# Identity products added into free PSUM banks on a TensorE-bound block of three layers, with banks taken ahead of the operands

## The reference, cut to what matters

```
S = S * w_t + (S a_t) b_t^T + v_t k_t^T ;   y_t = S r_t
```

## Time and profile before

| | |
|---|---|
| three runs | 4579.30, 4583.82, 4586.74 us, median 4583.82 |
| profiled execution | 4590.26 us, span 4588.4 us |
| granted TensorE clock, mean of the span | 0.847 |
| PE busy | 3906.6 us, 85% |
| DVE, ACT, POOL busy | 1815.2, 1229.7, 163.9 us |
| DMA | 219.39 MB, mean 48 GB/s |

### The profile page before, as it was taken

The page is one execution under the profiler, slowest core; times in us unless marked ns, Lnnn a source line. Parts: engine busy times, 40 slices in busy tenths (PEclk is TensorE's granted clock), DMA queues, the critical chain, the costliest instruction groups (busy, mean ns, idle before and its releaser), DMA issues. The chain is left out here.

```text
span 4588.4 us, 67812 instructions
## 1 busy us (share of the span) xinstructions
PE 3906.6 (85%) x29441; PEld 2998.5 (65%) x29441; DVE 1815.2 (40%) x2944; ACT 1229.7 (27%) x1936; POOL 163.9 (4%) x116
## 2 busy tenths in 40 slices
PE   5888888897888898999777667779799999877888
PEld 4667666677777798998455444558677877334543
DVE  3443444424444435343344344453553344322231
ACT  2222212212333222222222333322222221244230
POOL 0000000000000101000011001120000000000000
PEclk8777777759988798999887778779999999867987
DMA  3000000001111132332101001013223332201110
GB/s 128 16 16 15 16 16 16 16 2 56 29 32 33 45 104 65 92 90 67 37 24 37 28 24 32 22 44 97 69 75 95 93 92 87 69 10 32 37 33 23
DMA packets 58554, 219.39 MB, mean 48 GB/s; under 512 B 6608, under 2 KB 6608, under 8 KB 57616
## 3 DMA queue, kind: packets, MB, share of 16 engines
q1 hardware_dynamic: 57168, 211.37, 15.2%
q0 software_dynamic: 1088, 3.67, 0.2%
HBM read 210.83 MB, written 4.19 MB: 47 GB/s over the span
## 5 line engine op out<-in xcount | busy, mean ns | idle before, releaser
L385 PE MATMUL psum<-arena 32*32 32x32 f32 (+16 forms) x16392 | 1378.6, 265 | 529.8 <-DVE arena L321 152.1
L385 PE MATMUL psum<-arena,ring 128*128 128x264 f32 (+3 forms) x5152 | 1664.7, 414 | 18.3 <-DVE arena L330 11.8
L385 PEld LDWEIGHTS psum<-arena 32*32 32x32 f32 (+9 forms) x16392 | 988.6, 153 | 922.7 <-issue 332.3
L385 PE MATMUL psum<-arena,arena 128*128 128x264 f32 (+1 forms) x6336 | 1394.1, 328 | 74.7 <-DVE arena L321 37.3
L385 PEld LDWEIGHTS psum<-arena,ring 128*128 128x128 f32 (+2 forms) x5152 | 939.4, 199 | 371.6 <-issue 278.0
L385 PEld LDWEIGHTS psum<-arena,arena 128*128 128x128 f32 x6336 | 1004.2, 192 | 192.5 <-issue 62.1
L314 ACT ACTIVATE arena<-psum 128x512 f32<-128x512 f32 (+11 forms) x561 | 258.1, 460 | 1287.0 <-PE psum L385 1176.8
L321 DVE TENSOR_TENSOR ring<-ring,arena 128x1024 fp32r<-128x1024 f32 (+1 forms) x280 | 333.2, 1190 | 488.4 <-ACT arena L314 484.3
L321 DVE TENSOR_TENSOR arena<-arena 128x528 f32<-128x528 f32 (+9 forms) x700 | 336.8, 481 | 350.0 <-ACT arena L311 208.7
L314 ACT ACTIVATE arena<-ring 128x1024 fp32r<-128x1024 f32 (+1 forms) x280 | 286.7, 1024 | 558.5 <-PE psum L385 480.5
L321 DVE TENSOR_TENSOR arena<-arena,psum 88x192 f32<-88x192 f32 (+4 forms) x428 | 193.4, 452 | 585.9 <-PE psum L385 578.9
(11 more groups left out here) (24 smaller groups left out, 701.6 us busy)
## 6 DMA issues: line engine op xcount, KB each, us to landing
ring<-in_w SPq DMA_DIRECT2D x368, 512.0 KB, 3.5
ring<-in_w SPq DMA_DIRECT2D x24, 256.0 KB, 2.7
arena<-in_x SPq DMA_DIRECT2D x2, 2112.0 KB, 14.7
arena<-in_con SPq DMA_DIRECT2D x1, 3576.0 KB, 11.3
out<-arena SPq DMA_DIRECT2D x1, 2048.0 KB, 6.3
arena<-in_par SPq DMA_DIRECT2D x1, 1988.0 KB, 15.5
skew<-arena POOLq DMA_DIRECT2D x4, 320.0 KB, 2.6
arena<-skew POOLq DMA_DIRECT2D x4, 256.0 KB, 2.9
```

Source lines behind the costliest of these rows:

```text
L385: self.last_ins = self.eng.matmul(out, l, r, start=start, stop=stop, skip_group_check=skip)
```

## The change

A counter `idle` is kept while the program is written out; nothing of it runs on the chip. `mm` adds what a product is taken to last, the larger of 25 and n/2.4, and takes off n x rows/128, where n is the number of columns, times four for F32. `tr` adds 100. `wait_ge` adds 300 for each wait that is issued. The counter never goes below -1500 in `mm`. `bank` calls `warm` once the bank is free: while the counter is over 300 it issues a product of the 128x128 identity with itself into the first 128 columns of that bank, which the next real product overwrites. Each such product lowers the counter by 512 - 213.3 = 298.7.

The second part moves calls of `bank` ahead of waits on operands, in some 35 places: the wait on the bank, and what `warm` issues, then stand before the wait on the operand.

```diff
     def bank(self, n, *emptied):
...
         self.book.put(("bank",) + emptied, b)
+        self.warm(b)
         return b
+
+    def warm(self, b):
+        while self.idle > 300:
+            self.mm(self.ps[:, 512 * b:512 * b + 128], self.ident, self.ident)
+
+    def wait_ge(self, sem, n):
+        if self.seen.get(sem.num, 0) < n:
+            self.idle += 300
+        super().wait_ge(sem, n)
...
     def mm(self, out, l, r, start=True, stop=True, skip=False):
+        rows, n = l.shape[0], math.prod(r.shape[1:]) * (1 if r.dtype == F32R else 4)
+        self.idle = max(-1500, self.idle + max(25, n / 2.4) - n * rows / 128)
         self.last_ins = self.eng.matmul(out, l, r, start=start, stop=stop, skip_group_check=skip)
 
     def tr(self, out, a):
         n = a.shape[0]
+        self.idle += 100
         self.last_ins = self.eng.transpose(out, a, self.ident[0:n, 0:n])
...
     def prep(hp):
         for i, nme in enumerate("rkv"):
             s, w = P.slab((3 + 3 * hp + i) * SLAB, "rw_proj", hp, i)
+            b = P.bank(2, "rw_sh", hp, i)
             P.wait_ge(*landed(K, s))
-            b = P.bank(2, "rw_sh", hp, i)
             P.keep(b, 2)
...
-    def blocks(done, emptied, l, r):
+    def blocks(done, emptied, l, r, *needs):
         b = P.bank(1, *emptied)
+        for event in needs:
+            P.wait_ge(*at(*event))
...
         for l in (2, 4, 8, 16):
             for hh in range(2):
                 u = m.unit[hh]
-                P.wait_ge(*at("rw_mask", l, hp, hh))
-                P.wait_ge(*(at("rw_xt", l // 2, hp, hh)))
-                blocks(("rw_inv", "Y", l, hp, hh), ("rw_yp", l, hp, hh), u.M0 if l in (2, 8) else u.M1, u.Xp)
+                blocks(("rw_inv", "Y", l, hp, hh), ("rw_yp", l, hp, hh), u.M0 if l in (2, 8) else u.M1, u.Xp,
+                       ("rw_mask", l, hp, hh), ("rw_xt", l // 2, hp, hh))
             P.advance()
             for hh in range(2):
                 u = m.unit[hh]
-                P.wait_ge(*at("rw_yp", l, hp, hh))
-                blocks(("rw_inv", "Z", l, hp, hh), ("rw_x", l, hp, hh), u.XTp, u.Yp)
+                blocks(("rw_inv", "Z", l, hp, hh), ("rw_x", l, hp, hh), u.XTp, u.Yp, ("rw_yp", l, hp, hh))
                 blocks(("rw_inv", "ZT", l, hp, hh), ("rw_xt", l, hp, hh), u.Yp, u.XTp)
...
```

More of the change, by code:

```diff
@@ L356, in __init__ @@
         self.free, self.nbank, self.kept, self.slabs = [None] * 8, 0, set(), []
+        self.idle = 0.0
     def bank(self, n, *emptied):
@@ L1315, in project @@
         yield
+        b = P.bank(2, "df_V", hd)
         P.wait_ge(*at("df_v", hd))
-        b = P.bank(2, "df_V", hd)
         for j, (t0, tw) in enumerate(TK):
@@ L1352, in values @@
         nb = 2 if i == 4 else 1
+        b = P.bank(nb, "df_wt", hd, i)
         P.wait_ge(*at("df_w", hd, i))
-        b = P.bank(nb, "df_wt", hd, i)
         m0 = 512 * b if i == 4 else 512 * b + 128 * i
@@ L1864, in glin @@
         s, w = P.slab(off, *done)
+        b = P.bank(1, *emptied)
         P.wait_ge(*landed(K, s))
-        b = P.bank(1, *emptied)
         P.keep(b)
@@ L1886, in v_tile, with four @@
         P.drop(b)
-    def four(done, emptied, l, r):
+    def four(done, emptied, l, r, *needs):
         b = P.bank(1, *emptied)
+        for event in needs:
+            P.wait_ge(*at(*event))
         for J in J4:
@@ L1902, in pe_mixers @@
     s, w = P.slab(w0, "gd_small")
+    b = P.bank(1, "gd_lr")
     P.wait_ge(*landed(K, s))
-    b = P.bank(1, "gd_lr")
     for k in range(8):
@@ L1916, in delta @@
         yield
+        b = P.bank(1, "gd_to")
         P.wait_ge(*at("gd_g"))
-        b = P.bank(1, "gd_to")
         P.mm(bk(b)[:, 0:16], c["triu"], m.G["g"])
@@ L1922, in delta @@
         yield
+        b = P.bank(1, "gd_ct")
         P.wait_ge(*at("gd_bec"))
-        b = P.bank(1, "gd_ct")
         P.tr(bk(b)[0:16, 0:128], m.G["cu"])
@@ L1935, in delta @@
             yield
+            b = P.bank(1, "gd_diff", hd)
             P.wait_ge(*at("gd_ct"))
-            b = P.bank(1, "gd_diff", hd)
             for j in range(4):
@@ L1942, in delta @@
             yield
-            P.wait_ge(*at("gd_qi", hd))
-            four(("gd_kk", hd), ("gd_A", hd), U.k, U.k)
+            four(("gd_kk", hd), ("gd_A", hd), U.k, U.k, ("gd_qi", hd))
             four(("gd_kq", hd), ("gd_M", hd), U.k, U.q)
@@ L1954, in delta @@
             yield
+            b = P.bank(1, "gd_AT", hd)
             P.wait_ge(*at("gd_A", hd))
-            b = P.bank(1, "gd_AT", hd)
             for J in J4:
@@ L1988, in delta @@
             yield
+            b = P.bank(1, "gd_yp", 64, hd)
             P.wait_ge(*at("gd_m0", hd))
-            b = P.bank(1, "gd_yp", 64, hd)
             for j in range(4):
@@ L1995, in delta @@
             yield
+            b = P.bank(1, "gd_x64", hd)
             P.wait_ge(*at("gd_yp", 64, hd))
@@ L2013, in delta @@
                 if j:
+                    b = P.bank(1, "gd_us", j, hd)
                     P.wait_ge(*at("gd_wt", hd))
                     P.wait_ge(*at("gd_s", j, hd))
[L2016 removed]
                     P.mm(bk(b)[:, 0:128], U.wT[:, J], so)
@@ L2049, in decay_attention @@
         yield
+        b = P.bank(1, "la_ks", r)
         P.wait_ge(*at("la_qi", r))
-        b = P.bank(1, "la_ks", r)
         for J in J4:
@@ L2093, in linear @@
             off += 6 * SLAB
+            b = P.bank(1, "la_pre", r)
             P.wait_ge(*at("gd_lr"))
-            b = P.bank(1, "la_pre", r)
             P.mm(bk(b), p["glaw2"][0:16, 128 * r:128 * r + 128], m.LR[0:16])
@@ L2671, in pe_experts @@
             if e == 0:
+                b = P.bank(1, "r_ct")
                 P.wait_ge(*at("r_w"))
-                b = P.bank(1, "r_ct")
                 for j in range(4):
@@ L2943, in scores @@
             R, (k0, W) = slice(64 * r, 64 * r + 64), keys_of(kind, i)
+            b = P.bank(1, "fx_e", t, r, i)
             P.wait_ge(*at("fx_qk", t, "k"))
-            b = P.bank(1, "fx_e", t, r, i)
             s_ = bk(b)[:, 0:W]
@@ L2962, in values @@
             k0, W = keys_of(kind, i)
+            b = P.bank(1, "fx_a", t, r, i)
             P.wait_ge(*at("fx_p", t, r, i))
-            b = P.bank(1, "fx_a", t, r, i)
             for j in range(W // 128):
@@ L3012, in sticks @@
                 W = 512 - 128 * j
+                b = P.bank(1, "st_z", t, r, j)
                 P.wait_ge(*at("fx_k", t))
-                b = P.bank(1, "st_z", t, r, j)
                 P.mm(bk(b)[:, 0:W], d.k[R, J4[j]], d.q[R, 128 * j:512])
@@ L3019, in sticks @@
                 W = 512 - 128 * j
+                b = P.bank(1, "st_a", t, r, j)
                 P.wait_ge(*at("st_lk", t, r, 3))
-                b = P.bank(1, "st_a", t, r, j)
                 P.mm(bk(b)[:, 0:W], c["slo"], m.Lk[j][:, 0:W])
@@ L3052, in tables @@
         for i in range(8):
+            b = P.bank(1, "tb_v", i)
             P.wait_ge(*at("tb_rb", i))
-            b = P.bank(1, "tb_v", i)
             P.mm(bk(b), m.rb[0:32, 0:128], c["oh"][0:32])
```

16 lines of the change are left out of this document (5 added, 11 removed).

## The result

The changed kernel takes 4643.2 us (median of 4634.8, 4638.8, 4647.5 and 4650.0) against 4582.2 us of the kernel before in the same comparison: ratio 1.0131, 95% interval 1.0110 to 1.0152. It is slower by 61 us. The profiled execution took 4634.8 us, the lowest of its four; that of before, 4590.3, was the highest of its own. So the two traces differ by 45 us and the medians by 61. The two traces say where 45 us went.

A forecast was written before the change was run, and what follows sets the result against it. PE was taken to bound the kernel, busy 85% of the span, with 31% at half clock. Terms 25 + 6 + 8 + 0 + 0 = +39 us on 4590.3 gave 4629, as a median 4623 us; range 4550 to 4655.

The forecast's parts named there:

- Count: Whole kernel: 286 identity products, 572 records; 16 in each of head pairs 1 to 6, placed by the counter's rule.
- Price of one: One identity product: 0.22 us at full speed, 0.44 at half, plus 0.15 for a group among small blocks.
- Head pairs 1 to 6: RWKV's middle head pairs: each net 4.1 us longer, six times 25 us; bounds 14 and 38.
- give-back: Head pairs 1 to 6: work pushed behind the clock's rise runs in half the time, returning 2.2 us each.
- Head pair 0: First RWKV head pair: 29 products, nearly all at full speed, cost 6 us; bounds 4 and 9.
- Head pair 7: Last RWKV head pair: 68 products, levels at full speed but longer; +8 us, ends +14 and -4.
- What I doubted: Head pair 7: w2, u and chain, 26 us at half speed, might keep a raised clock; perhaps 10 us would go.
- Mixers: Mixers: 76 products fill waits and lift the clock, but shorten no round; 0 us, bounds +8 and -5.
- Moves of `bank`: `bank` calls moved ahead of operand waits: cost nothing, since both waits must end before the first product in either order.
- Rival (a): Gram products: clock held at full speed there, 10 us a head pair, 70 in seven; total 4553 us; chance 0.17.
- Rival (c): Nothing is given back in head pairs 1 to 6 and head pair 7 stays slow: +61, 4645 us; chance 0.15.
- what it would show: Signs: 30013 PE records, middle head pairs 4 us longer, chain and gram at 0.50, decay rounds 4.4 to 4.6 us at 1.00.

The follow-up runs named there:

- few rows: Changed kernel's 272 products in the same places, each with 32 rows of the identity instead of 128: 4699.5 us, ratio 1.0266 to the kernel before.
- gram few: Kernel before, moved banks, ten 32-row identity products ahead of the first `Ak` per head pair, no counter products: 4593.4 us against 4581.9, ratio 1.0025.
- no last: Changed kernel without the products from the first level to the last piece of the inverse in the last head pair: 4626.7 us, ratio 1.0109 to before.
- moves only: Changed kernel with counter and moved `bank` calls but no identity product issued: 4580.7 us against 4579.1 of the kernel before, ratio 1.0009.
- no mixers: Changed kernel without the products in the three mixers of block 2: 4623.3 us, ratio 1.0107 to the kernel before.
- gram fill: Kernel before, moved banks, ten full-row identity products ahead of the first `Ak` per head pair, no counter products: 4528.3 us against 4580.9, ratio 0.9882.
- rounds too: gram fill plus, in seven chains, 16 and 20 products at two waits and 5 in each later chunk: 4513.2 us against 4585.7 before, ratio 0.9828.

## Why the prediction was right, and where its steps were not

The sign and the mechanism held: products between PE's own work cost time, and their full rows give back about half of what the same products with few rows cost. The sum, 4623, was 20 us short of the median and inside the range. On the profiled execution it was 39 against 45, and that nearness comes from errors that cancel, and from a trace that was the fastest of its four runs.

- **Count.** 272 products, not 286: 14 or 15 per middle head pair instead of 16, 26 before the first chain, 71 in the last inverse, 78 from the mixers on to the experts. Counting along the old order shifted more of them than the "place at most" that I allowed.
- **Price of one.** Right at full speed, short for a group. In the last inverse a level has groups of 4, 2, 3, 1, 3 and 1 products that take 1.09, 0.64, 0.87, 0.42, 0.87 and 0.42 us: 0.22 for each and 0.20 for the group, where I had 0.22 and 0.15. At half speed the 32-row products of gram few start 0.43 us apart, against 0.44.
- **Head pairs 1 to 6: 25 forecast, 4 to 18 measured**: 727.5 in the changed kernel's trace and 737.8 in that of no last, which has the same products there, against 723.8 of before and 720.1 of moves only. So one pair of traces does not size this term; in both the forecast was too high. Without anything given back I had 38; few rows shows 24 to 27, with 85 products instead of 96, and there some clock is lost besides. The give-back, 2.2 us per head pair in the forecast, is 3.3 against the changed kernel's trace and 1.6 against no last's: half-speed time (the sums of the table's brackets) falls from 66.6 us to 58.6 and to 62.6.
- **Head pair 0: 6 forecast, 7 to 9 measured** (186.6 and 188.2 against 179.3), up to the upper bound. "Nearly all at full speed" holds for the 128-row products alone; with 32 rows in their place the stretch took 25 us more than before.
- **Head pair 7: 8 forecast, 16 measured** (119.6 against 103.8; 17.7 in the trace with them taken out). The level was given 6.4 us and took 7.27: one product more, 14 instead of 13, 0.20 instead of 0.15 for each of six groups, and 3.0 instead of 2.6 us for the six blocks at full speed. The larger error is how long the levels stayed slow: from Y evacuation to Y evacuation they took 11.60, 7.77 and 7.27 us where they had taken 5.38, 5.33 and 6.41, so the first two cost 6.2 and 2.4 us more, since the clock came up only at 992.0, in the second. From level 16's evacuation to the chain 5.8 us were added. What I doubted did not happen: w2, u and chain stayed at half speed, in the 44.3 us from 1015.9 on.
- **Mixers: 0 forecast, 16 measured.** This is the step that failed: "the products fill such waits" and "a faster PE shortens no round". The second is true, but the first was not held against the size of the wait. It is 0.97 us in the rows of before above; the changed kernel puts eight products (16 records) into that level, four ahead of the decay product and four between the inverse's blocks at half speed, where they push the next decay product back. In three groups they take 1.08, 0.73 and 1.58 us, 3.4 together, more than three times the wait. DVE lost 3.0 us there. By its instructions, in times of the kernel before, the losses lie in three places: 7 us between 2320 and 2363, 7 between 2498 and 2554, 4 between 2694 and 2710; no last repeats each of them within 0.2 us, and without the products (no mixers) they are gone. My upper bound of +8 was half of what came.
- **Moves of `bank`: nothing**, as forecast; moves only shows it.
- **Rival (a), the clock held at the gram products**, did not come about in the changed kernel, for the reason I gave: the counter places nothing in that wait. With products placed there it gives 9.0 us a head pair (120.0 to 111.0) where I had written 10, so its price was right. **Rival (c)**, 4645, had the right total by the wrong way: some 60 us were given back, on a larger cost.
- **Of what it would show**: 29985 records instead of 30013, middle head pairs 1 to 3 us longer instead of 4, chain and gram at 0.50, the last levels at 1.00 from the second on and longer, RWKV at 0.75. Decay rounds of 4.4 to 4.6 us at 1.00 failed where the inverse is beside them.
- **Two readings of the rows were off.** The row of the clock has a 5 and a 6 beside its 7 to 9. And the clock fell at 541.2, after the wait of 3.74 us and before that of 4.89, which begins later; only the first can have brought it down. Neither enters the sum.

On the Trainium skill's rule that the prediction weighed ("TensorE: Matmul & The Clock Gate", section on what is actually happening: the clock follows how busy the engine has been), the pair of gram fill and gram few decides: the same places, the same count, and 65 us between them when the rows drop from 128 to 32 (4528.3 and 4593.4). The same page of the Trainium skill, in its section on how the oscillation bites in real kernels, lays a fall to a wait of the engine. Gram fill goes that way, since filling a wait of 2.38 us held the clock through 64-row products, though that wait is shorter than those of the page's example; gram few does not, since there the clock fell without a wait. The measurement decides: work with few rows counts less.

What stays open: why the medians lie 16 us further apart than the profiled executions. The likeliest place is the six middle head pairs: the same products took 10.3 us more there in one trace than in another (737.8 and 727.5). Within one trace, too, like head pairs differ: in moves only, the levels take 42.9 to 48.7 us with 3.4 to 14.9 us of half speed, and its eleven runs spread over 19 us (4572.1 to 4590.8). That this explains the medians is not shown.

## What to carry to other kernels

Work added to hold TensorE's clock paid best where the engine waits anyway just before a long run of narrow products (53 us for 80 products; just behind the wait the same products gained 15). Look for the wait in the timeline at the place where the granted clock falls, and put full-row products there by hand. A counter that fires by the amount of narrow work puts them between the narrow products, where each costs 0.22 to 0.43 us and a change of form. And a rise of the clock is no gain by itself: in the chain half-speed time fell from 27 to 3 us for 1.2 us of time, since its start does not move with the clock and the products that held it took the time that it gave in the others. Last, compare more than one trace before you put a size to a term: two traces of the same instructions in the same six head pairs were 10 us apart.

## What the hardware showed that was not expected

- Narrow products kept a clock that they did not raise: 64- and 88-row products kept full speed for some 10 us once the wait ahead of them was filled (PE without a gap from 441.33 to 458.75), the same products that stay at half speed for 20.50 us when they begin there.
- Half-speed time in the levels varies between like head pairs of one run. In few rows, three head pairs have 0.0 us of it in the levels, with 32-row products only, and three have 11 to 12; so a difference of some us there between two traces need not be an effect of an edit. This is what misled me on the levels.
- Groups of identity products among 32x32 blocks cost 0.20 us for the group, whatever its size (0.42 us for one, 1.09 for four).
- Transposes alone raised the clock. In the first head pair of the kernel before, PE stood idle for 12.38 us, then ran 24 transposes with 128 rows and nothing else from 106.66 on, and the clock rose at 111.12, before the first product behind them; gram fill and rounds too show the same at 108.9.

```profile
106.66 4.98 PE L389 MATMUL psum<-arena 128*88 128x128 f32 x24 [12.38 <-DVE arena L321]
111.57 4.60 PE L385 MATMUL psum<-arena 64*32 64x32 f32 x118
```

```profile
107.70:111.12 3.42, 3.42 (x18) 3.16 (x17) 0.00 (x0) 1.91 (x3) 0.00 (x0) 0.50 0.00 0
111.12:115.00 3.88, 3.88 (x111) 3.59 (x110) 0.78 (x2) 2.09 (x4) 0.00 (x0) 1.00 0.02 4
```
